# Weight sums of a gate-and-up unit formed by GpSimd instead of VectorE, in a two-layer decoder step

## Chip, cores and metric

The kernel runs on one core of a Trainium2 chip. The metric is the device time of one execution in microseconds; three executions of a kernel are timed.

## What is computed

A step of a hybrid decoder with two layers, for a prompt of 512 tokens and 8 sequences of 8 sampled tokens, with 1024 features. Each layer is a half-step feed-forward, a mixer (three head groups) and a second half-step feed-forward. The change lies in the feed-forward, of which there are four:

```
def swiglu(h, w_in, w_out):
    gate, up = jnp.split(h @ w_in, 2, axis=-1)
    return (jax.nn.silu(gate) * up) @ w_out
...
h = modulate(rmsnorm(x, lp['norm_w'][0]), mod[:, 0], mod[:, 1])
x = x + FFN_RES * mod[:, 2] * swiglu(h, lp['ffn1_w_in'], lp['ffn1_w_out'])
```

`w_in` is 1024 x 5632, `w_out` 2816 x 1024, all in float32.

## The kernel before

**Precision.** Each float32 operand of a matmul is split into a high part (a copy that rounds) and a low part (the operand less the high part). A product is three matmuls: high by high, low activations by high weights, high activations by low weights (`products`, line 352). Most high parts are made by ScalarE and most low parts by VectorE.

**Tiling.** The 576 tokens are two halves of 288 columns (`HALF`). A *unit* is 128 columns of the gate and the same 128 of the up projection: 128 partitions x 2048 weights, loaded by SyncE in two pieces of 512 KB into one of two slots of `wslot` (`load_unit`, line 305). A feed-forward block has 22 such units, in two halves of 11 (`HF`); after each half come 8 units of the down projection. `PLAIN = 3` units of the first half are multiplied plainly. The other 19 use a scheme with seven products in place of eight: the weights of a unit are a 2 x 2 block matrix of quarters a11, a12, a21, a22 of 512 columns (`QW`), and P1, P2, P6, P7, P5, P4, P3 (in this order on TensorE, 12 matmuls each) multiply quarters and sums of them by prepared forms of the activations. Four sums of quarters are needed per unit, one after another.

**Order in a unit.** The order is written by hand for each engine, with semaphores; most units run in a loop of pairs (`pairs`, line 323). For unit n:
- ScalarE (`unit`): second gate's activation of unit n-1 (line 1330); high part of the last three quarters of n (1308), which waits for all four sums of n; a copy of P1's result (1324, which P6 waits for); the activation's high part (1317); high part of the first two quarters of n+1 (1303); two more copies (1324); high part of the two free sums of n+1 (1313), which waits for their three operations; the first gate's activation (1353).
- VectorE (`unit`): product of the second half of n-1 (1531); the three operations of `weight_sums` for n+1 (1502, 1504, 1506); low part of the rest of n (1483, counted by `w_split`, on which P5 of n and SyncE's load of n+2 wait); the activation's low part (1541); low part of the first two quarters of n+1 (1477, which P1 of n+1 waits for); `last_sum` of n+1 (1514), which overwrites a12 and so must follow it; three combinations of TensorE's results with the copies (1520), between them the low part of the sums of n+1 (1488, which P6 of n+1 waits for, and which frees `sums`); product of the first half of n (1527).
- TensorE (`up`) waits per product: P1 for `lo` and `fin`, P6 for `lo` and the first copy, P5 for `w_split` and the second copy, P4 for the third copy, P3 for the second combination.

**Opening of a block.** The activations are normalised and split (VectorE 833, 837; ScalarE 1357, 1366), the plain units run on TensorE, and VectorE forms the four differences T1 to T4 (`t_op`, 1620) and later their low parts (`low_t`, 1628), the plain units' products (`plain_act`, 1537) and the sums of the first unit of seven products. The first half's end does the same for the first unit of the second half, between the additions to x.

GpSimd has no work in a feed-forward block.

Of the kernel before, what the change touches and what calls it, by code (L numbers as in the profile page):

```python
# [17 lines left out]
ALU = mybir.AluOpType  # L18
# [11 lines left out]
DT = D // P  # L30
# [47 lines left out]
QW = KH * P  # L78
# [48 lines left out]
def program(nc, A, O):  # L127
    ctx = ExitStack()
    with ctx:
# [10 lines left out]
        def sem(name):  # L140
            if name not in stage_sems:
                stage_sems[name] = stage_ctx.enter_context(nc.semaphore(name))
            return stage_sems[name]
# [179 lines left out]
        def pairs(e, a, b, step):  # L323

            n = a
            if b - a >= 6:
                with e.Fori(0, (b - a) // 2) as i:
                    step(a, i)
                    step(a + 1, i)
                n = a + 2 * ((b - a) // 2)  # L330
            for m in range(n, b):
                step(m, 0)
# [170 lines left out]
        with ExitStack() as st:  # L503
# [15 lines left out]
            block = st.enter_context(nc.Block())  # L519
# [402 lines left out]
        PLAIN = 3  # L922
# [6 lines left out]
        def ffn_block(l, q, k, m_gate, n0, next_units, pending):  # L929
# [11 lines left out]
            if True:  # L941
# [9 lines left out]
                sums, snaps = region("sums", [P, 2 * QW])[:], region("snaps", [P, 4 * HALF])[:]  # L951
# [40 lines left out]
                hi, lo, s_ready = sem(q + "hi"), sem(q + "lo"), sem(q + "s_ready")  # L992
# [14 lines left out]
                def up_units(half):  # L1007
                    return n0 + half * (HF + DT), n0 + half * (HF + DT) + HF
# [8 lines left out]
                def tile_of(half, n, i):  # L1017
                    return n - up_units(half)[0] + half * HF + 2 * i
# [4 lines left out]
                def w_raw(n):  # L1023
                    return wslot[:, n % 2, :]

                def groups_of(g, m):

                    return 1 + 2 * (g - PLAIN) + m

                def raw_ready(e, n, i):  # L1030
                    e.wait_ge(w_ready[n % 2], 32 * (n // 2 + 1) + 32 * i)
# [19 lines left out]
                with nc.Block(no_gpsimd_drain=True) as block:  # L1051
                    @block.sync
                    def _(e):
# [24 lines left out]
                        for half in range(2):  # L1078
# [24 lines left out]
                            for k2 in range(2):  # L1103
                                if b + k2 < next_units:
                                    down(half, k2, DT // 2 - 1, lambda: load_unit(e, b + k2))
                                else:
                                    down(half, k2, DT // 2 - 1, lambda: None)

                    @block.tensor
                    def _(e):  # L1110
                        def plain(w, side, kt, at, h, bank, order=range(DT)):
# [362 lines left out]
                    def _(e):  # L1474
# [13 lines left out]
                            e.tensor_tensor(wqL[:, 2 * QW:4 * QW], sums, wqH[:, 2 * QW:4 * QW].bitcast(F32), ALU.subtract)\  # L1488
                                .then_inc(lo, 1)

                        def quarters(n):
                            return [w_raw(n)[:, m * QW:(m + 1) * QW] for m in range(4)]

                        def weight_sums(half, n, i):

                            g = tile_of(half, n, i)
                            v = 4 * (g - PLAIN)
                            a11, a12, a21, a22 = quarters(n)
                            raw_ready(e, n, i)
                            if not (isinstance(g, int) and g == PLAIN):  # L1500
                                e.wait_ge(lo, groups_of(g - 1, 2))
                            e.tensor_tensor(sums[:, QW:2 * QW], a11, a21, ALU.subtract).then_inc(s_ready, 1)
                            e.wait_ge(s_ready, v + 1)
                            e.tensor_tensor(a21, a21, a22, ALU.add).then_inc(s_ready, 1)
                            e.wait_ge(s_ready, v + 2)
                            e.tensor_tensor(sums[:, 0:QW], a21, a11, ALU.subtract).then_inc(s_ready, 1)

                        def last_sum(half, n, i):

                            g = tile_of(half, n, i)  # L1510
                            _, a12, _, _ = quarters(n)
                            e.wait_ge(s_ready, 4 * (g - PLAIN) + 3)
                            e.wait_ge(lo, groups_of(g, 1))
                            e.tensor_tensor(a12, a12, sums[:, 0:QW], ALU.subtract).then_inc(s_ready, 1)

                        def combine(out, bank, m, g, done, s_done):
                            u = g - PLAIN
                            e.wait_ge(prod, 6 * u + done)
# [26 lines left out]
                        def unit(half, n, i, opening=False, middle=None):  # L1545

                            g = tile_of(half, n, i)
                            u, s = g - PLAIN, unit_set(half, n)
                            if not opening:
                                second_half(g - 1)  # L1550
                            if middle is None:
                                weight_sums(half, n + 1, i)
                            lo_rest(n, i, groups_of(g, 2))
                            if not opening or half == 0:
                                low_act(g - 1, g - 1 - half * HF)
                            if middle is None:
                                lo_gate(n + 1, i, groups_of(g + 1, 1))
                                last_sum(half, n + 1, i)
                            combine(s1, s + 2, 1, g, 2, 1)
                            if middle:  # L1560
                                middle()
                            combine(s7, s, 2, g, 5, 3)
                            if middle is None:
                                lo_sums(groups_of(g + 1, 2))
                            combine(s2, s + 1, 3, g, 6, 2)
                            first_half(g)
# [71 lines left out]
                        t_op(T3, hB[1], hB[0])  # L1638
                        e.wait_ge(sem(q + "t_ops"), 2)
                        t_op(T4, hA[1], t_of(T2))  # L1640
                        weight_sums(0, n0 + PLAIN, 0)
                        e.wait_ge(group_done, groups_after(n0 + 1))
                        low_t(T2)
                        plain_act(1, 4)
                        lo_gate(n0 + PLAIN, 0, groups_of(PLAIN, 1))
                        last_sum(0, n0 + PLAIN, 0)
                        lo_sums(groups_of(PLAIN, 2))
                        low_t(T3)
                        low_t(T1)
# [38 lines left out]
                        for half in range(2):  # L1688
                            a, b = up_units(half)
                            if half == 0:  # L1690
                                a += PLAIN
                            unit(half, a, 0, opening=True)
                            pairs(e, a + 1, b - 1, lambda n, i: unit(half, n, i))
                            unit(half, b - 1, 0, middle=lambda: down_lo(e, b))
                            if half == 0 and early:
                                keep(-2)
                            second_half((half + 1) * HF - 1)
                            low_act((half + 1) * HF - 1, HF - 1)
                            a, b = down_units(half)
                            if half == 0:  # L1700
                                for k2 in range(2):
                                    if k2 == 0 and early:
                                        keep(-1)
                                    down_lo(e, a + 1 + k2)
                                    if k2 == 0 and early:
                                        e.wait_ge(mods_kept, early)
                                        finish_mods(e, Link(e, q + "gate_step"), (), 2)
                                    add(half, k2, 0)
                                with e.Fori(1, DT // 2 - 1) as i:
                                    for k2 in range(2):  # L1710
                                        down_lo(e, a + 1 + k2, i)
                                        add(half, k2, i)
                                down_lo(e, b - 1)
                                add(half, 0, DT // 2 - 1)
                                keep_block(0)
                                weight_sums(1, b, 0)
                                lo_gate(b, 0, groups_of(HF, 1))
                                last_sum(1, b, 0)
                                add(half, 1, DT // 2 - 1)
                                lo_sums(groups_of(HF, 2))  # L1720
                                keep_block(1)
                                continue
                            for d in range(DT - 2):
                                down_lo(e, a + d + 1)
                                add(half, d % 2, d // 2)
                                if d >= 2:
                                    add_square(e, q, d - 1)
                            add_square(e, q, DT - 3)
                            down_lo(e, b - 1)
                            tail_dve(e, q, m_gate, (2, 4), lambda d: e.wait_ge(sem(q + "first_done"), d - DT + 3),  # L1730
                                     lambda d: e.wait_ge(group_done, groups_after(a + d)), next_opening,
                                     lambda: keep_block(2))
                            keep_block(3)
# [10 lines left out]
        for l in range(DEPTH):  # L1744
# [33 lines left out]
            q = "mx_"  # L1778
# [1879 lines left out]
```

## Time and profile before

| | us |
|---|---|
| median of three runs | 2445.44 |
| lowest and highest | 2444.28, 2446.49 |
| span of the profiled execution | 2444.5 |
| TensorE busy | 2378.6 |
| VectorE busy | 1633.2 |
| ScalarE busy | 1041.9 |
| GpSimd busy | 11.4 |

The page gives no time of the profiled execution besides its span, from its first to its last instruction. Engines are PE (TensorE), PEld (its weight loads), DVE (VectorE), ACT (ScalarE), POOL (GpSimd) and SP (SyncE). L352 is line 352. A group's line gives operation, result and inputs by name, shapes and count, then the busy time in us and the mean of one in ns. A busy TensorE is not one at its peak, since matmuls overlap.

### The profile page before, as it was taken

The numbers are of one execution on the slowest core, as the hardware profiler recorded it, in microseconds if no ns is written. First come the engines' busy times: TensorE is split into PE (matmuls) and PEld (weight loads), VectorE is DVE, ScalarE is ACT, GpSimd is POOL, SyncE is SP. The second block draws the span as 40 slices with busy tenths as digits, with TensorE's granted clock in tenths as the row PEclk, the third lists the DMA queues.
The fourth block names the chain that finished last, engine by engine and source line by source line (L and its number), as shares of the span: only waits on it lengthen the run. The fifth ranks groups of instructions, "written<-read, shape, count | busy, mean of one in ns | idle before, by whom it ended". The sixth has DMA issues, their size and how long they took to land. (4 is left out here: it accounts for less than half of the span.)

```text
span 2444.5 us, 48393 instructions
## 1 busy us (share of the span) xinstructions
PE 2378.6 (97%) x18999; PEld 2240.0 (92%) x18999; DVE 1633.2 (67%) x2812; ACT 1041.9 (43%) x1723; POOL 11.4 (0%) x43
## 2 busy tenths in 40 slices
PE   7999999999999999999999999999999899999998
PEld 5998999899877999899999989988989789999997
DVE  7872684474877786278478538736668778846854
ACT  5541453242574554145255315414246645523532
POOL 0000000000000000000000000000000000000000
PEclk8999999999998999999999999999999999999998
DMA  8246335532233224623233463365121432333331
GB/s 297 88 127 220 119 103 175 187 92 71 73 122 106 70 74 136 228 89 98 83 87 86 155 199 89 103 226 165 45 91 53 147 99 58 98 89 91 88 88 63
DMA packets 367532, 285.84 MB, mean 117 GB/s; under 512 B 18273, under 2 KB 355479, under 8 KB 366982
## 3 DMA queue, kind: packets, MB, share of 16 engines
q1 hardware_dynamic: 366956, 283.36, 37.5%
q8 instruction: 115, 1.88, 0.3%
q14 instruction: 51, 0.42, 0.1%
q10 hardware_dynamic: 410, 0.18, 0.0%
HBM read 271.71 MB, written 11.79 MB: 116 GB/s over the span
## 5 line engine op out<-in xcount | busy, mean ns | idle before, releaser
L352 PE MATMUL PS<-f_xH,f_wqH 128*128 128x288 f32 x2140 | 635.0, 297 | 3.1 <-issue 3.0
L352 PE MATMUL PS<-f_xL,f_wqH 128*128 128x288 f32 x2140 | 632.2, 295 | 0.0
L352 PE MATMUL PS<-f_xH,f_wqL 128*128 128x288 f32 x2140 | 630.2, 294 | 0.0
L352 PEld LDWEIGHTS PS<-f_xH,f_wqH 128*128 128x128 f32 x2140 | 401.4, 188 | 5.9 <-issue 5.4
L352 PEld LDWEIGHTS PS<-f_xH,f_wqL 128*128 128x128 f32 x2140 | 403.4, 189 | 0.0
L352 PEld LDWEIGHTS PS<-f_xL,f_wqH 128*128 128x128 f32 x2140 | 401.9, 188 | 0.0
L352 PE MATMUL PS<-f_actH,f_wqH 128*128 128x288 f32 x1408 | 321.4, 300 | 1.3 <-DVE f_wqL L1048 1.3
L352 PE MATMUL PS<-f_actL,f_wqH 128*128 128x288 f32 x1408 | 315.6, 296 | 0.0
L352 PE MATMUL PS<-f_actH,f_wqL 128*128 128x288 f32 x1408 | 315.6, 296 | 0.0
L776 DVE SCALAR_TENSOR_TENSOR xT<-PS,modT,xT 128x288 f32<-128x288 f32 (+1 forms) x80 | 41.4, 517 | 359.7 <-PE PS L352 359.5
L352 PEld LDWEIGHTS PS<-f_actH,f_wqH 128*128 128x128 f32 x1408 | 230.8, 189 | 27.0 <-issue 25.0
L352 PEld LDWEIGHTS PS<-f_actL,f_wqH 128*128 128x128 f32 x1408 | 231.4, 189 | 0.2
L352 PEld LDWEIGHTS PS<-f_actH,f_wqL 128*128 128x128 f32 x1408 | 231.5, 189 | 0.0
L352 PE MATMUL PS<-mx_hH,in_wH 128*128 128x288 f32 x768 | 181.5, 308 | 8.2 <-DVE mx_hL L837 8.2
L1044 ACT ACTIVATE f_wqH<-wslot 128x1408 fp32r<-128x1408 f32 x64 | 87.9, 1373 | 203.2 <-PE PS L352 203.2
L352 PE MATMUL PS<-mx_hH,in_wL 128*128 128x288 f32 x768 | 172.7, 296 | 0.0
L352 PE MATMUL PS<-mx_hL,in_wH 128*128 128x288 f32 x768 | 172.3, 296 | 0.0
L1324 ACT ACTIVATE f_snaps<-PS 128x288 f32<-128x288 f32 x228 | 93.2, 409 | 136.7 <-PE PS L352 133.6
L1048 DVE TENSOR_TENSOR f_wqL<-wslot,f_wqH 128x1408 fp32r<-128x1408 f32 x64 | 104.0, 1625 | 55.7 <-ACT f_wqH L1044 54.2
L1483 DVE TENSOR_TENSOR f_wqL<-wslot,f_wqH 128x1536 fp32r<-128x1536 f32 x76 | 133.2, 1752 | 7.3 <-ACT f_wqH L1308 7.3
L352 PEld LDWEIGHTS PS<-mx_hH,in_wH 128*128 128x128 f32 x768 | 125.6, 190 | 12.8 <-issue 6.3
L1330 ACT ACTIVATE f_snaps<-PS 128x288 f32<-128x288 f32 x76 | 31.2, 411 | 236.0 <-PE PS L352 234.1
(562 smaller groups left out, 4282.8 us busy)
## 6 DMA issues: line engine op xcount, KB each, us to landing
wslot<-in_ffn_w_in SPq DMA_DIRECT2D x176, 512.0 KB, 5.0
masks<-in_w_mod SPq DMA_DIRECT2D x42, 1536.0 KB, 6.3
wslot<-in_ffn_w_out SPq DMA_DIRECT2D x64, 384.0 KB, 4.2
wslot<-in_w_in SPq DMA_DIRECT2D x48, 512.0 KB, 4.8
wslot<-in_ffn_w_out SPq DMA_DIRECT2D x64, 320.0 KB, 3.4
setup<-in_w_mod SPq DMA_DIRECT2D x6, 1536.0 KB, 13.3
wslot<-in_w_out SPq DMA_DIRECT2D x16, 512.0 KB, 4.6
dec<-in_cache_attn_k SPq DMA_DIRECT2D x16, 384.0 KB, 4.7
```

What stands on the lines that cost most here:

```text
L352: ins = e.matmul(outs[j], w, x_hl[j][part], start=(start and w is wh and part == 0), stop=(stop and w is wl), skip_group_check=True)
L776: return e.scalar_tensor_tensor(out=xd[:, 0:HALF], in0=PS[:, b, 0:HALF], scalar=mod_col(m, d), in1=xd[:, 0:HALF], op0=ALU.mult, op1=ALU.add)
L1044: e.activation(down_w(wqH, n), w_raw(n)[:, 0:HF * P], ACT.Copy).then_inc(w_hi, 1)
L1048: e.tensor_tensor(down_w(wqL, n), w_raw(n)[:, 0:HF * P], down_w(wqH, n).bitcast(F32), ALU.subtract)\
L1324: e.activation(dst, PS[:, bank, 0:HALF], ACT.Copy).then_inc(snap, 1)
L1330: e.activation(sgB, PS[:, unit_set(half, n), 0:HALF], ACT.Silu).then_inc(gate_ready, 1)
L1483: e.tensor_tensor(wqL[:, (3 + a) * QW:7 * QW], w_raw(n)[:, a * QW:4 * QW], wqH[:, (3 + a) * QW:7 * QW].bitcast(F32), ALU.subtract).then_in ...
```

## The change

In every feed-forward block a program for GpSimd is added, which forms the four sums of every unit with the same operations, the same semaphore (`s_ready`) and the same waits; it waits once at the start until all activations are whole. The same calls are removed from VectorE's program. GpSimd forms the sums of a unit as soon as its weights have been loaded and the low part of the preceding sums is made.

```
+                    @block.gpsimd
+                    def _(e):
+                        def quarters(n):
+                            return [w_raw(n)[:, m * QW:(m + 1) * QW] for m in range(4)]
+                        def weight_sums(half, n, i):
+                            g = tile_of(half, n, i)
+                            v = 4 * (g - PLAIN)
+                            a11, a12, a21, a22 = quarters(n)
+                            raw_ready(e, n, i)
+                            if not (isinstance(g, int) and g == PLAIN):
+                                e.wait_ge(lo, groups_of(g - 1, 2))
+                            e.tensor_tensor(sums[:, QW:2 * QW], a11, a21, ALU.subtract).then_inc(s_ready, 1)
+                            e.wait_ge(s_ready, v + 1)
+                            e.tensor_tensor(a21, a21, a22, ALU.add).then_inc(s_ready, 1)
+                            e.wait_ge(s_ready, v + 2)
+                            e.tensor_tensor(sums[:, 0:QW], a21, a11, ALU.subtract).then_inc(s_ready, 1)
+                        def last_sum(half, n, i):
+                            g = tile_of(half, n, i)
+                            _, a12, _, _ = quarters(n)
+                            e.wait_ge(s_ready, 4 * (g - PLAIN) + 3)
+                            e.wait_ge(lo, groups_of(g, 1))
+                            e.tensor_tensor(a12, a12, sums[:, 0:QW], ALU.subtract).then_inc(s_ready, 1)
+                        def all_sums(half, n, i):
+                            weight_sums(half, n, i)
+                            last_sum(half, n, i)
+                        for half in range(2):
+                            a, b = up_units(half)
+                            if half == 0:
+                                a += PLAIN
+                                e.wait_ge(sem(q + "h_whole"), 2 * DT)
+                            all_sums(half, a, 0)
+                            pairs(e, a + 1, b, lambda n, i: all_sums(half, n, i))
...
                             if not opening:
                                 second_half(g - 1)
-                            if middle is None:
-                                weight_sums(half, n + 1, i)
                             lo_rest(n, i, groups_of(g, 2))
                             if not opening or half == 0:
                                 low_act(g - 1, g - 1 - half * HF)
                             if middle is None:
                                 lo_gate(n + 1, i, groups_of(g + 1, 1))
-                                last_sum(half, n + 1, i)
                             combine(s1, s + 2, 1, g, 2, 1)
...
                         t_op(T4, hA[1], t_of(T2))
-                        weight_sums(0, n0 + PLAIN, 0)
                         e.wait_ge(group_done, groups_after(n0 + 1))
                         low_t(T2)
                         plain_act(1, 4)
                         lo_gate(n0 + PLAIN, 0, groups_of(PLAIN, 1))
-                        last_sum(0, n0 + PLAIN, 0)
                         lo_sums(groups_of(PLAIN, 2))
...
                                 keep_block(0)
-                                weight_sums(1, b, 0)
                                 lo_gate(b, 0, groups_of(HF, 1))
-                                last_sum(1, b, 0)
                                 add(half, 1, DT // 2 - 1)
                                 lo_sums(groups_of(HF, 2))
```

## Rows read from the trace of the kernel before

**Rows 1.** The page, busy time of the engines and its share of the span.

```profile
PE 2378.6 (97%) x18999; PEld 2240.0 (92%) x18999; DVE 1633.2 (67%) x2812; ACT 1041.9 (43%) x1723; POOL 11.4 (0%) x43
```

**Rows 2.** Who waited for whom, TensorE alone: us in total, times, longest.

```profile
PE PS L352 <- issue: 5.6, 6, 1.3
```

**Rows 3.** Busy time of the engines in six units, first block: stretch, engines, clock, DMA.

```profile
102.60:169.80 67.20, 67.20 (x506) 67.20 (x505) 57.01 (x79) 35.25 (x55) 0.00 (x0) 1.00 0.38 113
```

**Rows 4.** Groups of VectorE by line and shape, whole span.

```profile
L1483 DVE TENSOR_TENSOR f_wqL<-wslot,f_wqH 128x1536 fp32r<-128x1536 f32 x76 | 133.2, 1752 | 7.3 <-ACT f_wqH L1308 7.3
...
L1477 DVE TENSOR_TENSOR f_wqL<-wslot,f_wqH 128x1024 fp32r<-128x1024 f32 x80 | 97.4, 1218 | 6.7 <-ACT f_wqH L1303 6.7
L1488 DVE TENSOR_TENSOR f_wqL<-f_sums,f_wqH 128x1024 fp32r<-128x1024 f32 x76 | 92.4, 1216 | 0.0
...
L1506 DVE TENSOR_TENSOR f_sums<-wslot 128x512 f32<-128x512 f32 x76 | 52.6, 692 | 2.6
...
L1541 DVE TENSOR_TENSOR f_actL<-rms,f_actH 128x576 f32 x56 | 42.0, 750 | 0.0
L1531 DVE TENSOR_TENSOR rms<-f_snaps 128x288 f32<-128x288 f32 x76 | 34.9, 459 | 73.8 <-ACT f_snaps L1330 73.8
```

**Rows 5.** Timeline of VectorE in one unit: start, us, engine, line, operation.

```profile
155.03 1.22 DVE L1488 TENSOR_TENSOR f_wqL<-f_sums,f_wqH 128x1024 fp32r<-128x1024 f32 x1
...
156.80 0.46 DVE L1527 TENSOR_TENSOR rms<-f_snaps 128x288 f32<-128x288 f32 x1
158.21 0.46 DVE L1531 TENSOR_TENSOR rms<-f_snaps 128x288 f32<-128x288 f32 x1 [0.95 <-ACT f_snaps L1330]
...
160.64 1.75 DVE L1483 TENSOR_TENSOR f_wqL<-wslot,f_wqH 128x1536 fp32r<-128x1536 f32 x1
...
164.30 0.69 DVE L1514 TENSOR_TENSOR wslot<-wslot,f_sums 128x512 f32<-128x512 f32 x1
```

**Rows 6.** Timeline of ScalarE in the same unit.

```profile
157.76 0.41 ACT L1330 ACTIVATE f_snaps<-PS 128x288 f32<-128x288 f32 x1 [3.04 <-PE PS L352]
158.07 1.48 ACT L1308 ACTIVATE f_wqH<-wslot 128x1536 fp32r<-128x1536 f32 x1
159.45 0.41 ACT L1324 ACTIVATE f_snaps<-PS 128x288 f32<-128x288 f32 x1
...
164.47 1.05 ACT L1313 ACTIVATE f_wqH<-f_sums 128x1024 fp32r<-128x1024 f32 x1
```

**Rows 7.** Timeline of SyncE's issues there; the page's landing time of such loads.

```profile
151.31 1.00 SPq L305 DMA_DIRECT2D wslot<-in_ffn_w_in  x2
...
wslot<-in_ffn_w_in SPq DMA_DIRECT2D x176, 512.0 KB, 5.0
```

**Rows 8.** Groups of GpSimd by line and shape, and a self-wait in its timeline.

```profile
L2850 POOL MEMSET dec<- 128x1536 f32 x2 | 2.8, 1382 | 0.0
...
L550 POOL TENSOR_SCALAR_AFFINE_SELECT ident<-ident 128x128 f32<-128x128 f32 x1 | 0.3, 292 | 0.2 <-POOL masks L549 0.2
...
L558 POOL TENSOR_SCALAR_AFFINE_SELECT bsel<-bsel 64x8 f32<-64x8 f32 x1 | 0.2, 185 | 0.1
...
3.88 0.29 POOL L550 TENSOR_SCALAR_AFFINE_SELECT ident<-ident 128x128 f32<-128x128 f32 x1 [0.24 <-POOL masks L549]
```

**Rows 9.** Opening of the first block: timelines of VectorE, ScalarE and TensorE; a tile's row.

```profile
71.45 0.75 DVE L1537 TENSOR_TENSOR rms<-PS,f_snaps 128x576 f32<-128x576 f32 x1
...
85.83 3.89 DVE L1628 TENSOR_TENSOR f_xL<-f_tb,f_xH 128x1152 fp32r<-128x1152 f32 x3
...
90.52 0.76 DVE L1537 TENSOR_TENSOR rms<-PS,f_snaps 128x576 f32<-128x576 f32 x1
...
91.37 0.41 ACT L1324 ACTIVATE f_snaps<-PS 128x288 f32<-128x288 f32 x1 [0.80 <-DVE rms L1537]
...
91.88 0.37 PE L352 MATMUL PS<-f_xH,f_wqH 128*128 128x288 f32 x1 [0.75 <-issue]
...
L352 PEld LDWEIGHTS PS<-f_xH,f_wqH x2140: 185/188/193, 74.9 to 2352.0; 128*128 128x128 f32 x195
```

More of the change, by code:

```diff
@@ L1489, in lo_sums @@
                                 .then_inc(lo, 1)
[L1491 to L1514, printed above, removed]
                         def combine(out, bank, m, g, done, s_done):
```

## The prediction

> **What bounds the kernel now.** I read the page first: TensorE is busy for 2378.6 of the 2444.5 us of the profiled span [rows 1], so nothing that another engine saves counts unless TensorE waits for it. Next the waits of TensorE: of the feed-forward's groups only small ones are there, and the one that this change can reach is the 5.6 us put down to "issue", 6 times [rows 2]. Then the table of stretches for six gate-and-up units: 67.20 us, TensorE busy for 67.20 at full clock, VectorE for 57.01, ScalarE for 35.25, GpSimd for nothing [rows 3]. So a unit lasts 11.20 us (84 matmuls, 7 products of 1.6 us), TensorE has no hole in it, and VectorE's 9.5 us a unit are hidden. 76 units have weight sums (8 in the first and 11 in the second half of each of four blocks).
>
> The timelines give the deadlines in one such unit. Its first product starts near 157.6 (the second gate's activation is released at 157.76 by the product before) [rows 6]. Then P6 starts at 160.8, P5 at 164.0, P3 at 167.2, the next unit at 168.8. The copy for P6 ends at 159.86, 0.9 us early [rows 6]. The low part of the rest, which P5 waits for, runs from 160.64 to 162.39, 1.6 us early [rows 5]. The three sums lie ahead of it, right behind the product at 158.21 [rows 5], and are wanted only by ScalarE at 164.47 [rows 6]; the fourth runs at 164.30 [rows 5] and is wanted at the next unit's large copy, 11.2 us after 158.07, so at 169.27 [rows 6].
>
> **What is removed.** Four subtractions or additions of 0.69 us in 76 units: 76 x 4 x 0.692 = 210 us of VectorE [rows 4]. In the units that is worth nothing: TensorE is full there [rows 3]. It moves the low part of the rest from 160.64 to about 159.65, when its high part (158.07 + 1.48) is there, and the load behind it as much. The load of the next unit was issued at 151.31 and takes some 5.0 us [rows 7], so it is in the slot by about 156.8 (its second piece follows half a us later), and GpSimd can start then or a little earlier.
>
> The openings are different. In the first block VectorE makes three low parts from 85.83 to 89.72, then an activation's low part, then the third plain unit's product at 90.52; ScalarE's copy follows at 91.37 and TensorE resumes at 91.88 after 0.75 us [rows 9]. The same hole stands once in each of the four blocks. Four sums (2.7 us) leave VectorE's queue ahead of the three low parts; they cannot start before the fourth one's place, so 0.6 us of this is gained: the product at 89.95, the copy at 90.8, TensorE at 91.3. Gain 4 x 0.57 = 2.3 us, at most 4 x 0.75 = 3.0, if GpSimd disturbs nothing.
>
> **What is added: the price of a sum on GpSimd.** The trace has no GpSimd operation with two inputs, so this is bounded by its nearest rows. A one-input select of 128 columns takes 292 ns, of 8 columns 185 ns: 0.89 ns a column and 0.18 us fixed; a memset of 1536 columns takes 1382 ns, 0.9 ns a column [rows 8]. If all streams overlap, 512 columns cost 0.18 + 0.46 = 0.64 us; if two reads and the write follow one another, 0.18 + 3 x 0.46 = 1.55. I take the two reads one after the other with the write beside them, 1.1 us, because the select (one read, one write) costs hardly more a column than the memset (write alone), so a write is free and a read is not. The hop from one own instruction to a waiting one is 0.24 us [rows 8]. Three sums are then 3 x 1.1 + 2 x 0.24 = 3.8 us: from 156.8 to 160.6, against ScalarE's 164.47; the fourth from about 163.4 to 164.5, against 169.27. If the two engines do not disturb each other, 3.6 us of slack stand in front of every unit even at 1.55 us. The Trainium skill, GPSIMD Engine Reference, section Performance versus the Vector engine, gives 4497 ns for such an operation of 2048 columns at about 2.6 cycles an element; its estimate for 512 columns would be about 1.2 us. It would change nothing in the sum.
>
> **What is added: two engines at the same memory.** No row shows GpSimd reading while VectorE runs a two-input operation, so this is bounded too: from no interference (0) to complete exclusion. For exclusion I add the two-input operations of VectorE that stay in a unit: 1.75 + 1.22 + 1.22 + 0.75 + 0.46 + 0.46 = 5.86 us [rows 4] (the last two are the products of the halves, lines 1531 and 1527, of one shape). With four sums of 1.1 that is 10.3 us, with eight changes of owner of some 0.04 (an estimate from VectorE's start at 158.21 [rows 5], 0.04 us after the activation that it waited for ends at 157.76 + 0.41 [rows 6]; GpSimd's own hop lies beside VectorE's turn) 10.6, below 11.2. Walked through with alternating turns: sum 1 from 156.5 to 157.6; the first half's product, now at 156.80 [rows 5], ends at 158.1, so the copy for P6 ends at 160.2 instead of 159.86, still before 160.8; sum 2 to 159.2; the second half's product (now 158.21) to 159.6; sum 3 to 160.7; the low part of the rest 160.7 to 162.4, as today; the fourth sum 164.3 to 165.4, before VectorE's next two-input operation, 11.2 us after 155.03, so at 166.23 [rows 5]. TensorE stays full. The Trainium skill, SBUF — State Buffer, section Who interferes with whom, says just this: a VectorE instruction with two SBUF inputs and a GpSimd instruction that reads SBUF exclude each other for the whole instruction. No run here shows it; it is the rule that speaks against this change.
>
> With exclusion the openings lose instead of gain. GpSimd may begin once the sixteen input tiles are whole (about 67.3, estimated from the place of the T operations just ahead of the product at 71.45), in the middle of VectorE's four T operations. Two sums get in ahead of the first plain unit's product, which today ends at 71.45 + 0.75 = 72.2; with three sums and VectorE's turns it ends at 75.5 to 75.8, and TensorE wants it at 74.9 [rows 9]. Later the fourth sum falls among the three low parts and pushes them by 1.1, of which 0.6 is paid by the sums that left. Together I walk the resumption at 91.88 to about 93.0: +1.15 us in each of four blocks, +4.6. The second halves' openings come out even: one sum in front of the low part of the rest instead of three.
>
> **Other edits at nothing.** GpSimd's queue holds nothing else in a feed-forward block, so nothing is delayed behind its waits. No DMA is moved; SyncE's loads follow the low part of the rest, which is no later. The loop and wait instructions of GpSimd lie in its own idle time.
>
> **The sum.** Without exclusion: 2444.5 - 2.3 = 2442.2 us; with it: 2444.5 + 4.6 = 2449.1. The page has no time for the profiled execution but its span; the median 2445.4 is 0.9 above it. I take the second, less a little for openings in which GpSimd finds a free turn: **2449 us**, a loss that is just inside what can be told from no change (0.2%, 4.9 us).
>
> **Rivals.** (1) No interference: 2443 us (2442.2 + 0.9). For it: only that no row shows any. Against: both need two reads a column. (2) Slower, by one mechanism: exclusion and a sum longer than about 1.3 us. Place: the chain sum 1, first half's product, second gate, high part of the rest, copy, P6 in every unit, and the fourth sum against the low part of the sums at 166.23. A unit becomes 5.86 + 4p + 0.3, so it passes 11.2 at p = 1.26 to 1.3. 68 units have both a predecessor's chain and a successor's sums. p = 1.4: +0.56 x 68 = 38 us, less if a turn falls well (the combines, 0.46 us each three times a unit, need no second read of this memory), so 2465 to 2485; at the bound 1.55: +1.15 x 68 = 78, 2528. For it: the margin is 0.6 us of 11.2, and the real hand-over is unknown. Against: the price by rows is 1.1. (3) Faster by over 0.2%: openings give at most 3.0 us, and 4.9 are needed; it would take a hole that these views don't show.
>
> **Chances.** Units hidden: 0.55, of which 0.28 with exclusion (the forecast) and 0.27 without interference (rival 1). Rival 2: 0.40. Rival 3: 0.05. Since the small loss with exclusion ends close to 4.9 us, a part of it is slower: faster 0.05, within 0.2% 0.50, slower 0.45. If the units are hidden, the range is 2441 to 2452; to hold 8 in 10 it must reach into rival 2: **2441 to 2485**.
>
> **What would show it.** Right: six units still 67.2 us with TensorE full; VectorE's share down by some 200 us; GpSimd's sums near 1.1 us when alone; VectorE's two-input operations lengthened or late where a sum runs; the hole at each opening longer than 0.75 us. No interference: VectorE's durations unchanged and the hole at 0.2 us. Rival 2: a unit's period over 11.2 us, with TensorE's P6 waiting for ScalarE's copy. It would be wrong altogether if ScalarE waited for GpSimd's sums at the high part, or if the span fell by over 4.9 us.

## The result and the profile after

| | before | after |
|---|---|---|
| median, us | 2445.97 (4 runs) | 2472.17 (4 runs, 2471.59 to 2477.69) |
| span of the profiled execution, us | 2444.5 | 2475.6 |
| ratio to before | | 1.0116, 95% interval 1.0101 to 1.0131 |

The change makes the kernel slower by 26 us in the medians; the ratio of the runs gives 1.2%. This is inside the range of the prediction and 23 us from its number; the case that it held likeliest was "within 0.2%". It comes out at the time of the second rival, but not by its mechanism: the units are as fast as before, and nearly the whole loss arises at the four openings. Two slow executions, one of the ten of the run below with both units' sums held back (2969 us, mean clock 0.73) and one of the kernel before in the second set of runs (6476 us), are left out of the ratios and counted in the medians (without its slow one the first of these has 2449.60 us).

The page of the kernel after, busy time and share of the span:

```profile
PE 2392.4 (97%) x18999; PEld 2250.1 (91%) x18999; DVE 1606.8 (65%) x2508; ACT 1040.4 (42%) x1723; POOL 496.8 (20%) x347
```

Against [rows 1] TensorE is busy 13.8 us longer for the same 18999 matmuls, and idle for 2475.6 - 2392.4 = 83.2 us instead of 65.9. So the 31 us of span are 17.3 us of idle time and 13.8 us of slower work. The profiled execution is the longest of the four; the spans of the other three are 2469.6 to 2470.3 us, 5.3 to 6.0 us shorter. TensorE's waits (us in total, times, longest) say where the first part is:

```profile
PE PS L352 <- issue: 20.1, 6, 4.4
...
PE PS L352 <- DVE rms L1551: 3.5, 4, 0.9
```

The 5.6 us of [rows 2] have become 20.1, still 6 times, and a wait of 0.9 us for a plain unit's product has come up four times. 14.5 + 3.5 = 18.0 us: that is the idle time (the rest of the waits is 0.7 less, by subtraction).

The units, by the same stretch of six as [rows 3]:

```profile
102.60:169.80 67.20, 67.20 (x510) 66.03 (x509) 50.81 (x53) 34.33 (x54) 33.82 (x23) 1.00 0.35 103
```

TensorE is full. VectorE has only 6.2 us less work in six units, not the 16.6 us (24 x 0.692) that were taken from it. The groups of VectorE show why (lines are those of the changed file: 1522 was 1483, 1555 was 1541, 1545 and 1541 were 1531 and 1527):

```profile
L1522 DVE TENSOR_TENSOR f_wqL<-wslot,f_wqH 128x1536 fp32r<-128x1536 f32 x76 | 171.5, 2256 | 35.8 <-ACT f_wqH L1347 35.3
...
L1555 DVE TENSOR_TENSOR f_actL<-rms,f_actH 128x576 f32 x56 | 70.5, 1258 | 0.0
L1545 DVE TENSOR_TENSOR rms<-f_snaps 128x288 f32<-128x288 f32 x76 | 66.1, 870 | 47.9 <-ACT f_snaps L1369 47.4
L1541 DVE TENSOR_TENSOR rms<-f_snaps 128x288 f32<-128x288 f32 x76 | 58.8, 773 | 7.6 <-DVE f_snaps L1534 1.1
```

The two-input operations of [rows 4] are longer: the low part of the rest 2256 ns instead of 1752, the activation's low part 1258 instead of 750, the halves' products 870 and 773 instead of 459. VectorE's combinations, which take one input from TensorE's results, are not: 453 ns, before 455. Over the span VectorE gives up 210 us of sums and its busy time falls by 26.4. The sums themselves on GpSimd:

```profile
L1126 POOL TENSOR_TENSOR f_sums<-wslot 128x512 f32<-128x512 f32 x76 | 153.8, 2023 | 6.0
...
L1134 POOL TENSOR_TENSOR wslot<-wslot,f_sums 128x512 f32<-128x512 f32 x76 | 102.0, 1342 | 262.5 <-DVE f_wqL L1516 261.6 <-POOL f_sums L1126 0.9
```

The four sums have the same shape and cost 1342 to 2023 ns on average (1423 and 1600 for the two that are not shown): most of the difference is waiting. One unit shows it, VectorE first, then GpSimd:

```profile
151.63 1.13 DVE L1541 TENSOR_TENSOR rms<-f_snaps 128x288 f32<-128x288 f32 x1
153.11 1.12 DVE L1545 TENSOR_TENSOR rms<-f_snaps 128x288 f32<-128x288 f32 x1 [0.35 <-ACT f_snaps L1369]
154.61 2.39 DVE L1522 TENSOR_TENSOR f_wqL<-wslot,f_wqH 128x1536 fp32r<-128x1536 f32 x1 [0.38 <-ACT f_wqH L1347]
...
151.15 1.29 POOL L1122 TENSOR_TENSOR f_sums<-wslot 128x512 f32<-128x512 f32 x1 [1.74 <-DVE f_wqL L1527]
152.52 1.39 POOL L1124 TENSOR_TENSOR wslot<-wslot 128x512 f32<-128x512 f32 x1
153.99 1.40 POOL L1126 TENSOR_TENSOR f_sums<-wslot 128x512 f32<-128x512 f32 x1
158.88 1.30 POOL L1134 TENSOR_TENSOR wslot<-wslot,f_sums 128x512 f32<-128x512 f32 x1 [3.50 <-DVE f_wqL L1516]
```

The last sum runs while VectorE makes a combination and then waits, and takes 1.30 us: that is its price. The first three run in turns with VectorE. GpSimd's first ends at 152.44, and VectorE's product, 0.46 us when alone, issued at 151.63, ends at 152.76; the second ends at 153.91, VectorE's next product at 154.23; the third ends at 155.39 and the 1.75 us operation issued at 154.61 ends at 157.00, 1.6 us later. So an operation that meets the other engine's waits until that is done and then takes its own time less some 0.14 us, which pass during the wait: 0.32 us behind the sum for the product of 0.46, 1.61 for the operation of 1.75, and on GpSimd 1.15 (152.76 to 153.91) for a sum of 1.30. The hop from one sum to the next is 0.08 us. ScalarE's second gate is issued 11.12 and 11.20 us apart here, as before.

The opening of the first block, VectorE, GpSimd and TensorE:

```profile
86.15 7.20 DVE L1639 TENSOR_TENSOR f_xL<-f_tb,f_xH 128x1152 fp32r<-128x1152 f32 x3
93.27 1.81 DVE L1555 TENSOR_TENSOR f_actL<-rms,f_actH 128x576 fp32r<-128x576 f32 x1
95.22 0.76 DVE L1551 TENSOR_TENSOR rms<-PS,f_snaps 128x576 f32<-128x576 f32 x1
...
85.24 2.15 POOL L1134 TENSOR_TENSOR wslot<-wslot,f_sums 128x512 f32<-128x512 f32 x1 [11.25 <-DVE f_wqL L1516]
87.35 2.41 POOL L1122 TENSOR_TENSOR f_sums<-wslot 128x512 f32<-128x512 f32 x1
89.84 2.29 POOL L1124 TENSOR_TENSOR wslot<-wslot 128x512 f32<-128x512 f32 x1
92.21 2.26 POOL L1126 TENSOR_TENSOR f_sums<-wslot 128x512 f32<-128x512 f32 x1
...
96.58 0.58 PE L352 MATMUL PS<-f_xH,f_wqH 128*128 128x288 f32 x1 [4.38 <-issue]
96.96 0.44 PE L352 MATMUL PS<-f_xL,f_wqH 128*128 128x288 f32 x1
```

The first row of VectorE answers to its row at 85.83 in [rows 9]: three low parts took 3.89 us and take 7.20, the activation's low part 1.81 instead of 0.75, and the product of the third plain unit comes at 95.22 instead of 90.52. GpSimd stands beside them with four operations, not with one: the last sum of the first unit *and the three sums of the second unit*. TensorE resumes at 96.58 after 4.38 us instead of at 91.88 after 0.75. And its matmuls are then 0.24 us apart instead of 0.13. The table of stretches (busy times of the engines, granted clock, share of DMA) shows the clock in the eighth column:

```profile
94.00:96.00 2.00, 0.00 (x0) 0.00 (x0) 1.87 (x3) 0.00 (x0) 0.47 (x1) 1.00 0.00 0
96.00:98.00 2.00, 1.42 (x6) 1.45 (x7) 2.00 (x2) 1.93 (x3) 0.00 (x0) 0.53 0.00 0
98.00:100.00 2.00, 2.00 (x12) 2.00 (x12) 1.81 (x3) 0.22 (x1) 0.48 (x1) 0.61 0.41 116
```

TensorE stood idle for 4.4 us, up to 96 at a clock of 1.00; the two stretches behind show 0.53 and 0.61, its lower level of 1.2 GHz for most of them, and at 100 it is full again. The other three openings have a hole of the same length, but TensorE works at the lower level for longer behind two of them. Behind the third:

```profile
1314.00:1316.00 2.00, 2.00 (x10) 2.00 (x9) 2.00 (x3) 0.93 (x1) 0.00 (x0) 0.50 0.03 9
1316.00:1318.00 2.00, 2.00 (x11) 2.00 (x10) 0.74 (x2) 0.41 (x1) 1.27 (x1) 0.50 0.94 273
```

In the stretches of clock 0.50 behind the four holes (they begin at 96.1, 891.4, 1311.3 and 2099.8 us) TensorE is busy for 2.9, 3.0, 4.6 and 5.8 us; half of their sum, 8.1 us, is an estimate of what the clock costs there. The other 5.7 of the 13.8 us do not belong to the openings. Most of them lie in the mixers, where the change has no instruction: TensorE works there at half clock for 39.9 us in all, before for 26.2, in several stretches. How long they are changes from run to run. The longest such stretch of the changed kernel, and that of a run below which has no long hole at any opening (the last one under "The hole that was there before"):

```profile
772.00:789.00 17.00, 17.00 (x73) 9.69 (x70) 16.33 (x43) 7.65 (x12) 0.00 (x0) 0.50 0.36 106
...
765.60:782.60 17.00, 17.00 (x73) 9.75 (x70) 16.34 (x43) 7.60 (x12) 0.00 (x0) 0.50 0.35 105
```

So the openings account for 17.3 + 8.1 = 25.4 us, about the 26 us between the medians, and the rest of the 31 us of span is about what the profiled execution is longer than the other three.

### The profile page after: what moved, and what is told of

Its sections match the earlier page's. It is cut to its first block and busy times, and to the rows that moved or that the text cites. A ratio compares the mean times of both kernels' runs of the same rounds, so it can differ in the third digit from the quotient of the medians.

```text
span 2475.6 us, 48469 instructions
## 1 busy us (share of the span) xinstructions
PE 2392.4 (97%) x18999; PEld 2250.1 (91%) x18999; DVE 1606.8 (65%) x2508; ACT 1040.4 (42%) x1723; POOL 496.8 (20%) x347
## 5 line engine op out<-in xcount | busy, mean ns | idle before, releaser
L1122 POOL TENSOR_TENSOR f_sums<-wslot 128x512 f32<-128x512 f32 x76 | 108.2, 1423 | 933.8 <-ACT f_hf L1405 458.4
L1522 DVE TENSOR_TENSOR f_wqL<-wslot,f_wqH 128x1536 fp32r<-128x1536 f32 x76 | 171.5, 2256 | 35.8 <-ACT f_wqH L1347 35.3
L1534 DVE TENSOR_TENSOR f_snaps<-PS,f_snaps 128x288 f32<-128x288 f32 x228 | 103.1, 453 | 88.9 <-PE PS L352 87.9
L1363 ACT ACTIVATE f_snaps<-PS 128x288 f32<-128x288 f32 x228 | 93.2, 409 | 156.9 <-PE PS L352 139.2
L1126 POOL TENSOR_TENSOR f_sums<-wslot 128x512 f32<-128x512 f32 x76 | 153.8, 2023 | 6.0
```

The costliest lines, as they stand in the source:

```text
L1363: e.activation(dst, PS[:, bank, 0:HALF], ACT.Copy).then_inc(snap, 1)
L1522: e.tensor_tensor(wqL[:, (3 + a) * QW:7 * QW], w_raw(n)[:, a * QW:4 * QW], wqH[:, (3 + a) * QW:7 * QW].bitcast(F32), ALU.subtract).then_in ...
L1534: e.tensor_tensor(out, PS[:, bank, 0:HALF], out, ALU.add).then_inc(comb, 1)
```

## Experiments

Two theories. **Openings:** the loss is made at the four openings, by the sums beside VectorE's last low parts, and made half as large again by the clock. **Units:** sharing costs 0.3 to 0.4 us in each of the 68 units, and the openings are a small part.

### The second unit's sums held back

```
                             all_sums(half, a, 0)
+                            if half == 0:
+                                e.wait_ge(fin, 2 * PLAIN)
                             pairs(e, a + 1, b, lambda n, i: all_sums(half, n, i))
```

> GpSimd waits, in each block's first half, for the third plain unit's product before it forms the sums of the second unit; all else as in the changed kernel. Theory O (the loss is made at the four openings: three sums of the second unit and one of the first share the memory with VectorE's last low parts, 0.75 us of hole become 4.4, and TensorE's clock falls behind it): the three sums leave the low parts' stretch, the hole falls to some 1.2 us, the clock stays at full; 3.5 us stay from the wait for the first plain unit's product (0.7 to 0.9 us a block). So about 2451 us (2448 to 2455). Theory U (sharing in the 68 units costs some 0.3 to 0.4 us each, the openings are a small part): the time stays above 2460 us.

Measured: 2452.54 us, ratio 1.0029 (1.0017 to 1.0042). VectorE's three low parts, and TensorE after the hole:

```profile
84.39 5.00 DVE L1641 TENSOR_TENSOR f_xL<-f_tb,f_xH 128x1152 fp32r<-128x1152 f32 x3
...
91.55 0.37 PE L352 MATMUL PS<-f_xH,f_wqH 128*128 128x288 f32 x1 [1.10 <-issue]
```

5.00 us instead of 7.20, a hole of 1.10 us instead of 4.38, and no fall of the clock there (1.00 from 80 to 100 us). Three quarters of the loss are gone with one wait in each block, and nothing was taken from GpSimd. The wait for the first plain unit's product stays (3.5 us in all), and the four holes are 1.4 us above [rows 2]. The theory of the units falls.

### The first unit's sums held back too

```
                                 e.wait_ge(sem(q + "h_whole"), 2 * DT)
+                                e.wait_ge(fin, 2)
                             all_sums(half, a, 0)
+                            if half == 0:
+                                e.wait_ge(fin, 2 * PLAIN)
```

> As the run before, and the first unit's sums also wait until the first plain unit's product is made. Theory O: the wait of 0.7 to 0.9 us ahead of the third plain unit goes too, 2448 us (2446 to 2451). Theory U: above 2459 us.

Measured: 2450.19 us, ratio 1.0016 (1.0007 to 1.0026). The wait for the first plain unit's product is no longer among TensorE's waits; the group of holes is at

```profile
PE PS L352 <- issue: 6.8, 6, 1.3
```

which is 4 x 0.3 above [rows 2], the one sum that is left among the low parts. The two ratios differ by 0.0013 with overlapping intervals: the step has the expected sign and size (3.5 us are 0.0014), but the runs alone would not show it; the wait in the trace does.

### The first unit's sums on VectorE

```
                         t_op(T4, hA[1], t_of(T2))
+                        weight_sums(0, n0 + PLAIN, 0)
...
                         lo_gate(n0 + PLAIN, 0, groups_of(PLAIN, 1))
+                        last_sum(0, n0 + PLAIN, 0)
...
                                 e.wait_ge(sem(q + "h_whole"), 2 * DT)
-                            all_sums(half, a, 0)
+                            if half == 0:
+                                e.wait_ge(fin, 2 * PLAIN)
+                            else:
+                                all_sums(half, a, 0)
```

(The functions that were removed from VectorE's program are back in it.)

> The first unit's four sums of each block are formed by VectorE again, where they were, and GpSimd begins with the second unit behind the third plain unit's product; 72 of the 76 units' sums stay on GpSimd. Theory O: the openings are those of the kernel before, hole 0.75 us, so its time: 2446 us (2444 to 2449). Theory U: some 26 us of the loss stay, above 2460 us.

Measured: 2444.67 us, ratio 1.0003 (0.9991 to 1.0016). TensorE's holes, and the six units:

```profile
PE PS L352 <- issue: 5.6, 6, 1.3
...
102.60:169.80 67.20, 67.20 (x506) 67.20 (x505) 53.02 (x55) 35.15 (x55) 34.64 (x23) 1.00 0.38 113
```

The holes are those of [rows 2], the units those of [rows 3]. 72 of 76 units have their sums on GpSimd, and no cost or gain can be told (the interval goes from 2 us less to 4 us more). (A wait of 0.4 or 0.2 us has come up at P5 of the second unit in three blocks, for the low part of the rest, 0.8 us in all.)

### The same, with GpSimd running ahead

The last edit without its wait for `fin`.

> As the run before, but GpSimd forms the second unit's sums as soon as the first unit's have been split, beside VectorE's last three low parts. Theory O: three sums of 1.3 us push the low parts by 3 to 3.9 us in every block, the hole is about 4 us and the clock falls behind it, so most of the loss is back though the first unit is VectorE's: 2462 to 2472 us. A rival to it, that the loss came from the fourth sum in the low parts or from the first three in the T operations: 2448 us. Theory U: no difference from the run before.

Measured: 2464.11 us, ratio 1.0078 (1.0063 to 1.0092). Three low parts, TensorE after the hole, its holes, and the page's busy times:

```profile
85.33 6.09 DVE L1667 TENSOR_TENSOR f_xL<-f_tb,f_xH 128x1152 fp32r<-128x1152 f32 x3
...
94.65 0.58 PE L352 MATMUL PS<-f_xH,f_wqH 128*128 128x288 f32 x1 [4.01 <-issue]
...
PE PS L352 <- issue: 18.7, 6, 4.0
...
PE 2387.5 (97%) x18999; PEld 2248.2 (91%) x18999; DVE 1589.8 (65%) x2524; ACT 1040.2 (42%) x1723; POOL 464.7 (19%) x331
```

19 us, three quarters of the loss, are back by nothing but the time at which three sums of the second unit are formed. The hole is 4.01 us, the same in all four blocks. Against the run before it TensorE's holes are 18.7 - 5.6 = 13.1 us longer, and its busy time is up 7.2 us. Its work at half clock behind the four holes, 14.7 us, half of which is extra, accounts for that. So the fourth sum and the first three were the small parts, and the second unit's sums the large one.

### What excludes what: write only, and one read

The first three sums of each block's first unit are replaced by memsets of the same places, and by copies (both leave these sums out of the computation). One of the three, as memset and as copy:

```
-    e.tensor_tensor(sums[:, QW:2 * QW], a11, a21, ALU.subtract)
+    e.memset(sums[:, QW:2 * QW], 0.0)
```

```
-    e.tensor_tensor(sums[:, QW:2 * QW], a11, a21, ALU.subtract)
+    e.tensor_copy(sums[:, QW:2 * QW], a11)
```

> The changed kernel with the first three sums of each block's first unit replaced by memsets of the same places (these sums are left out of the computation, so its output differs). If GpSimd's reading is what excludes VectorE's two-input operations: the memsets take 0.53 us and the low part and T operations beside them their own 1.22, 1.35 and 1.35 us (2.32, 2.45 and 2.34 beside the sums), and the wait ahead of the third plain unit is gone. If any GpSimd operation at the same memory excludes them, they are lengthened by some 0.5 us each.

> The same with copies (one read, one write) in place of the three sums (left out of the computation). If one read is enough to exclude: each of the three VectorE operations beside a copy is lengthened by about the copy's own time, 0.6 us by the rows of the one-input select. If only two reads do: 1.22, 1.35 and 1.35 us.

One execution each, 2467.68 and 2467.19 us. VectorE's low part and two T operations, and GpSimd's three memsets beside them:

```profile
67.61 1.22 DVE L1639 TENSOR_TENSOR f_wqL<-wslot,f_wqH 128x1024 fp32r<-128x1024 f32 x1
68.75 1.35 DVE L1645 TENSOR_TENSOR f_tb<-f_hf 128x1152 f32<-128x1152 f32 x1
70.14 1.36 DVE L1645 TENSOR_TENSOR f_tb<-f_hf,f_tb 128x1152 f32<-128x1152 f32 x1
...
67.26 0.53 POOL L1143 MEMSET f_sums<- 128x512 f32 x1 [59.75 <-ACT f_hf L1419]
67.85 0.53 POOL L1145 MEMSET wslot<- 128x512 f32 x1
68.44 0.53 POOL L1147 MEMSET f_sums<- 128x512 f32 x1
```

The same with copies:

```profile
67.33 1.63 DVE L1639 TENSOR_TENSOR f_wqL<-wslot,f_wqH 128x1024 fp32r<-128x1024 f32 x1
68.88 1.76 DVE L1645 TENSOR_TENSOR f_tb<-f_hf 128x1152 f32<-128x1152 f32 x1
70.67 1.65 DVE L1645 TENSOR_TENSOR f_tb<-f_hf,f_tb 128x1152 f32<-128x1152 f32 x1
...
66.97 0.91 POOL L1143 COPY f_sums<-wslot 128x512 f32<-128x512 f32 x1 [59.49 <-ACT f_hf L1419]
67.94 1.49 POOL L1145 COPY wslot<-wslot 128x512 f32<-128x512 f32 x1
69.49 1.62 POOL L1147 COPY f_sums<-wslot 128x512 f32<-128x512 f32 x1
```

Beside memsets VectorE takes 1.22, 1.35 and 1.36 us, as alone, and GpSimd 0.53. Beside copies it takes 1.63, 1.76 and 1.65 us, 0.3 to 0.4 us more each, and the copies 0.91, 1.49 and 1.62. With the sums of the kernel after it was 2.32, 2.45 and 2.34. The ends of the copies show turns again: the second ends at 69.43, 0.47 us behind VectorE's low part (68.96), and the third at 71.11, 0.47 us behind the next operation (70.64). So a GpSimd operation that only writes does not hold up VectorE's two-input operations, one read is enough to exclude, and the price goes with the length of the GpSimd operation. I had expected 0.6 us beside a copy, from the select's rows.

### How near the units are to their limit

```
+    e.tensor_tensor(sums[:, 0:QW], a21, a11, ALU.subtract).then_inc(sem(q + "extra"), 1)
+    e.wait_ge(sem(q + "extra"), g - PLAIN)
     e.tensor_tensor(sums[:, 0:QW], a21, a11, ALU.subtract).then_inc(s_ready, 1)
```

in the version with the first unit on VectorE: a fifth operation in each of the 72 units on GpSimd.

> The version with each block's first unit on VectorE and the rest on GpSimd, with the third sum formed twice in each of the 72 units (the same result, one more operation of 1.3 to 1.4 us in the chain). If a unit is near its limit by complete exclusion, VectorE's two-input operations and GpSimd's sums add up: 5.86 + 5 x 1.3 = 12.4 us against 11.2, up to 1.2 us a unit, 2460 to 2525 us. If the units have room (turns fall beside VectorE's waits and its combinations with TensorE's results), 2446 to 2452 us.

Measured: 2472.49 us, ratio 1.0105 (1.0053 to 1.0158; two runs). VectorE, GpSimd, and ScalarE's wait for GpSimd:

```profile
143.54 2.31 DVE L1521 TENSOR_TENSOR f_wqL<-wslot,f_wqH 128x1024 fp32r<-128x1024 f32 x1
...
140.31 2.70 POOL L1126 TENSOR_TENSOR f_sums<-wslot 128x512 f32<-128x512 f32 x1
...
144.80 1.06 ACT L1357 ACTIVATE f_wqH<-f_sums 128x1024 fp32r<-128x1024 f32 x1 [1.08 <-POOL f_sums L1128]
```

VectorE takes 2.31 us for a 1.22 us operation and GpSimd 2.70 for a 1.3 us one, in turns without a gap, and ScalarE now waits for a sum. 26 to 28 us over 72 units are 0.37 us a unit for one more operation of about 1.4 us in the way. So the units had about 1 us of room with four sums (an estimate: 1.4 less 0.37), and units made longer by exclusion, as the second rival has it, exist, one operation further on. The place is another than the rival's: ScalarE's high part of the two free sums waits for GpSimd, 71.5 us in 48 waits. The mean granted clock is 0.990, before 0.989: many short waits, no fall.

### The hole that was there before

In the kernel before, VectorE makes `low_t(T3)` ahead of the first unit's first low part, where it stands idle, instead of behind it:

```
                         plain_act(1, 4)
+                        low_t(T3)
                         lo_gate(n0 + PLAIN, 0, groups_of(PLAIN, 1))
                         last_sum(0, n0 + PLAIN, 0)
                         lo_sums(groups_of(PLAIN, 2))
-                        low_t(T3)
                         low_t(T1)
```

> The kernel before with one move: the low part of T3 is made ahead of the first unit's first low part, where VectorE stands idle for 2.1 us, instead of among the last three. If VectorE's queue sets the hole of 0.75 us in each opening, 1.27 us leave it: hole 0.1 us or none, 4 x 0.6 to 0.75 = 2.4 to 3 us, 2443 us. If the hole is set by ScalarE's activation instead: 2446 us.

Measured: 2440.13 us against 2444.75, ratio 0.9981 (0.9970 to 0.9993). VectorE's last low parts, now two, and TensorE's holes:

```profile
86.32 2.62 DVE L1628 TENSOR_TENSOR f_xL<-f_tb,f_xH 128x1152 fp32r<-128x1152 f32 x2
...
PE PS L352 <- issue: 2.6, 2, 1.3
```

Four holes, 5.6 - 2.6 = 3.0 us, are gone, as much as the span's gain (2444.5 to 2441.5), and the ratio's interval (1.7 to 7.3 us) holds it. This is faster than both kernels, by 0.2% and 1.3%, with nothing on GpSimd.

> The same move in the version with the first unit's sums on VectorE and the others on GpSimd: 2443 us if the sums on GpSimd in the units cost nothing, over 2446 if they do.

Measured: 2443.0 us, ratio 0.9988 (0.9979 to 0.9997): the same move with 72 units' sums on GpSimd. It beats the kernel before as well, and its interval overlaps that of the run above, so putting the sums on GpSimd shows neither gain nor cost here.

## Why the prediction was right and wrong

- **TensorE full in the units, VectorE's 210 us worth nothing:** right, shown by the six-unit stretch and by the version with 72 units on GpSimd (1.0003). One sign was given wrongly: VectorE's share was to fall by some 200 us. Its busy time fell by 26.4, because the profile shows its waits for GpSimd as longer operations.
- **The price of a sum:** 1.1 us by rows, 1.30 measured; the taken bound was low by 0.2 and both ends (0.64, 1.55) held. The hop was taken as 0.24 us and is 0.08. The slack of 3.6 us "even at 1.55 us" does not follow from its own numbers: three sums of 1.55 from 156.8 end at 161.9, 2.5 us ahead of 164.47. Nothing else hung on it.
- **Exclusion:** taken as the case, and it is one. Operations take turns, and memsets, which only write, do not take part (1.22, 1.35 and 1.36 us beside them, as alone). By the Trainium skill, SBUF — State Buffer, section Who interferes with whom, a VectorE instruction with two SBUF inputs contends with a GpSimd instruction that reads SBUF and not with one that only writes it. The trace agrees.
- **5.86 + 4p + 0.3:** with the measured 1.30 this gives 11.36 us, over 11.2, and a loss of 11 us that is not there. That sum was too high because it counted all four sums against VectorE; the fourth runs at 158.88 beside VectorE's combination and its wait. The walk by turns, in the same part, was nearer.
- **The openings, +1.15 us each:** here the forecast failed. Its first half was good: the first plain unit's product was walked to 75.5 to 75.8 and ended at 75.87, and TensorE waited 0.7 to 0.9 us for it. But "the fourth sum falls among the three low parts and pushes them by 1.1" left out who stands behind it in GpSimd's queue. On VectorE the second unit's three sums were issued behind the third plain unit's product, at 91.20. On GpSimd their only waits are the weights and the low part of the first unit's sums, and both are met ahead of the low parts. They went in front of what the product waits for: TensorE resumed at 96.58 and not at 93.0. With these three sums held back (the first experiment) the terms that the walk did have come out at 3.5 + 1.4 = 4.9 us over the four blocks, against 4.6 forecast; the term that it lacked is 4.38 - 1.10 = 3.3 us of hole in each block, and the clock behind it.
- **The clock:** no term of the sum had it. At the openings it did not fall behind holes of 0.75 and 1.10 us, and it did behind those of 4.0 and 4.4. It costs about 8 us there.
- **The second rival** gave 2465 to 2485 us and the time is in it, but its mechanism did not decide: no unit passes 11.2 us steadily. The size of the range was owed to it, so the range held for another reason than the one it was drawn for, which is luck.

## What to carry to other kernels

An operation that is moved to an engine of its own loses not only its place but its lateness: whatever its old queue held it behind must be named (here its running ahead cost 19 of the 26 us), and if the new engine shares a resource with the old one, a wait has to stand for it. Look at the stretches where the engine that is to be relieved decides, not at its mean share: here four places of some 10 us each held nearly the whole result, and a reordering there (an idle gap used for one low part) was worth more than 210 us of moved work.

## What the runs showed of the hardware

- Two-input operations of VectorE and reading operations of GpSimd took turns, one operation each; the change of owner cost nothing that could be seen (0.32 us from the end of a sum to the end of a 0.46 us product). The trace shows the wait as a longer operation, not as idle time. Busy time of such an engine is then not all work: VectorE's fell by 26 us where 210 us of work were taken away.
- Memsets on GpSimd, 0.53 us for 512 columns, left VectorE's operations as they were.
- A 128 x 512 float32 operation with two inputs takes 1.29 to 1.30 us on GpSimd when VectorE has no such operation beside it, and 0.69 on VectorE.
- At the openings TensorE worked for some 3 to 6 us at half clock behind a hole of 4.0 to 4.4 us, matmuls 0.24 us apart for 0.13; behind holes of 1.1 us and below it did not. In the mixers its clock also fell, in both kernels, and for how long changed from run to run.
